# Delta levels: the upper chunk's products issued one PSUM bank behind the lower chunk's

## The reference, cut to what matters

```
a = jnp.einsum('bhnid,bhnjd->bhnij', k_beta, kc) * decay_strict
t_inv = lax.linalg.triangular_solve(eye + a, eye, left_side=True, lower=True, unit_diagonal=True)
u = t_inv @ (vc * bc[..., None])
w = t_inv @ (k_beta * jnp.exp(G)[..., None])
```

## Time and profile before

| | us |
|---|---|
| median of 3 executions | 2875.41 |
| lowest and highest | 2873.04, 2876.01 |
| the profiled execution, its own time | 2876.07 |
| its span, first to last instruction | 2874.3 |
| TensorE busy in the span | 2748.0 (96%) |
| VectorE, ScalarE, GpSimd busy | 1494.7, 967.8, 189.0 |
| mean granted TensorE clock | 0.972 |

### The profile page before, as it was taken

How to read it: one execution, slowest core, us unless ns; L and a number is a source line. 1 busy time by engine, 2 the same in 40 slices (tenths; PEclk the granted TensorE clock), 3 DMA queues, 4 the chain that set the end, 5 groups by cost and what they waited for, 6 DMA issues and landing times.

```text
span 2874.3 us, 42222 instructions
## 1 busy us (share of the span) xinstructions
PE 2748.0 (96%) x17756; PEld 2240.7 (78%) x17756; DVE 1494.7 (52%) x1845; ACT 967.8 (34%) x1471; POOL 189.0 (7%) x267
## 2 busy tenths in 40 slices
PE   6999999999999999999999899999999999968998
PEld 5888877687888878888777878888877777658787
DVE  6565565756565443333457644333365546755534
ACT  3222334523222332222345333222324444323322
POOL 3000000320000000000002300000010000013000
PEclk9999999989999999999999989999999999969999
DMA  7565542103566222232222012232232222100132
GB/s 287 200 218 203 191 167 72 52 18 112 202 207 220 88 85 102 86 112 88 95 80 71 3 59 90 88 108 93 90 103 74 66 74 69 61 1 3 56 103 73
DMA packets 46521, 299.68 MB, mean 104 GB/s; under 512 B 5664, under 2 KB 5792, under 8 KB 18080
## 3 DMA queue, kind: packets, MB, share of 16 engines
q1 hardware_dynamic: 37152, 230.35, 23.5%
q0 software_dynamic: 9216, 67.11, 6.5%
HBM read 295.35 MB, written 2.10 MB: 103 GB/s over the span
## 4 chain that ended last, share of the span: by engine, by line
PE 92%; DVE 5%; ACT 1%; DMA 1%; issue 1%; POOL 0%; SPq 0%; DVEq 0%; ACTq 0%
PE ps L921 18%; PE ps L922 18%; PE ps L923 18%; PE ps L1209 6%; PE ps L1210 6%; PE ps L1211 6%; PE ps L1516 2%; PE ps L1517 2%; PE ps L1518 2%; PE ps L2071 1%; PE ps L2055 1%; PE ps L2068 1%; DMA ada_first<-in_ada 1%; PE ps L1331 1%; PE ps L1295 1%
## 5 line engine op out<-in xcount | busy, mean ns | idle before, releaser
L921 PE MATMUL ps<-hn_hi,w_hi 128*128 128x512 f32 x1440 | 564.5, 392 | 16.9 <-DVE hn_lo L870 16.7
L922 PE MATMUL ps<-hn_lo,w_hi 128*128 128x512 f32 x1440 | 563.4, 391 | 0.0
L923 PE MATMUL ps<-hn_hi,w_lo 128*128 128x512 f32 x1440 | 562.9, 391 | 0.0
L897 DVE TENSOR_TENSOR w_lo<-w_raw,w_hi 128x2048 fp32r<-128x2048 f32 (+2 forms) x227 | 467.8, 2061 | 162.8 <-ACT w_hi L890 162.8
L890 ACT ACTIVATE w_hi<-w_raw 128x2048 fp32r<-128x2048 f32 (+2 forms) x227 | 390.6, 1721 | 100.0 <-PE ps L1211 97.3
L1209 PE MATMUL ps<-hn_hi,w_hi 128*128 128x512 f32 x776 | 323.6, 417 | 7.7 <-DVE hn_lo L870 4.9
L921 PEld LDWEIGHTS ps<-hn_hi,w_hi 128*128 128x128 f32 x1440 | 272.3, 189 | 75.3 <-issue 18.6
L923 PEld LDWEIGHTS ps<-hn_hi,w_lo 128*128 128x128 f32 x1440 | 272.3, 189 | 57.4
L922 PEld LDWEIGHTS ps<-hn_lo,w_hi 128*128 128x128 f32 x1440 | 272.4, 189 | 56.3
L1210 PE MATMUL ps<-hn_lo,w_hi 128*128 128x512 f32 x776 | 306.4, 395 | 0.0
L1211 PE MATMUL ps<-hn_hi,w_lo 128*128 128x512 f32 x776 | 305.8, 394 | 0.0
(11 more groups left out here) (470 smaller groups left out, 3630.9 us busy)
## 6 DMA issues: line engine op xcount, KB each, us to landing
w_raw<-in_up SPq DMA_DIRECT2D x88, 1024.0 KB, 4.9
ada_w<-in_ada POOLq DMA_DIRECT2D x64, 1024.0 KB, 5.2
w_raw<-in_down SPq DMA_DIRECT2D x64, 704.0 KB, 4.1
w_raw<-in_mix_in SPq DMA_DIRECT2D x20, 1024.0 KB, 4.9
w_raw<-in_dsa_in SPq DMA_DIRECT2D x18, 1024.0 KB, 4.9
w_raw<-in_merge SPq DMA_DIRECT2D x16, 768.0 KB, 4.3
ada_first<-in_ada SPq DMA_DIRECT2D x8, 1024.0 KB, 12.4
w_raw<-in_mix_out SPq DMA_DIRECT2D x8, 1024.0 KB, 4.9
```

What stands on the lines that cost most here:

```text
L897: dve.tensor_tensor(w_lo[:, slot, 0:size], w_raw[:, slot, 0:size], w_hi[:, slot, 0:size].bitcast(F32), ALU.subtract).then_inc(w_lo_ready, 1)
L921: pe.matmul(bank, wh, x_hi[:, k], start=(k == 0), stop=False)
L922: pe.matmul(bank, wh, x_lo[:, k], start=False, stop=False)
L923: return pe.matmul(bank, wl, x_hi[:, k], start=False, stop=(k == K - 1))
```

## The change

Both level functions now go over five steps instead of four. In step q the lower chunk's products of bank q and the upper chunk's products of bank q - 1 are issued in turn. The waits for bank q stand at the head of step q, so that they also stand before the upper products of bank q - 1. The increment that tells a bank is complete follows the upper chunk's last product of that bank, in step q + 1. Step 0 has lower products alone, step 4 upper products alone. Which products are made, their operands, their banks and the number of increments are the same. The other engines' programs are the same.

```
-            for q in range(4):
-                pe.wait_ge(delta_bt_ready, 2 * i + q // 2 + 1)
-                if m:
-                    pe.wait_ge(delta_xy_ready, 4 * (i - 1) + q + 1)
-                else:
-                    pe.wait_ge(delta_start, 2 * G + q // 2 + 1)
+
+            def product(q, j, c):
+                return pe.matmul(ps[half(c), level_bank(q), j * HD:(j + 1) * HD], d.bt[half(c), m % 2, q, j],
+                                 d.xy[half(c), q, j, 0], start=True, stop=True)
+            for q in range(5):
+                if q < 4:
+                    pe.wait_ge(delta_bt_ready, 2 * i + q // 2 + 1)
+                    if m:
+                        pe.wait_ge(delta_xy_ready, 4 * (i - 1) + q + 1)
+                    else:
+                        pe.wait_ge(delta_start, 2 * G + q // 2 + 1)
                 for j in range(2):
-                    for c in range(2):
-                        last = pe.matmul(ps[half(c), level_bank(q), j * HD:(j + 1) * HD], d.bt[half(c), m % 2, q, j],
-                                         d.xy[half(c), q, j, 0], start=True, stop=True)
-                last.then_inc(delta_v1_summed, 1)
+                    if q < 4:
+                        product(q, j, 0)
+                    if q:
+                        last = product(q - 1, j, 1)
+                if q:
+                    last.then_inc(delta_v1_summed, 1)
...
-            for q in range(4):
-                pe.wait_ge(delta_v1_ready, 4 * i + q + 1)
+            for q in range(5):
+                if q < 4:
+                    pe.wait_ge(delta_v1_ready, 4 * i + q + 1)
                 for j in range(2):
-                    at = P + j * P
                     if m < LEVELS - 1:
-                        for c in range(2):
-                            pe.matmul(ps[half(c), level_bank(q), at:at + HD], d.xy[half(c), q, j, 1], d.v1[half(c), q, j],
-                                      start=True, stop=True)
-                    for c in range(2):
-                        last = pe.matmul(ps[half(c), level_bank(q), at + HD:at + 2 * HD], d.v1[half(c), q, j], d.xy[half(c), q, j, 1],
-                                         start=True, stop=True)
-                last.then_inc(delta_xy_summed, 1)
+                        if q < 4:
+                            x_product(q, j, 0)
+                        if q:
+                            x_product(q - 1, j, 1)
+                    if q < 4:
+                        y_product(q, j, 0)
+                    if q:
+                        last = y_product(q - 1, j, 1)
+                if q:
+                    last.then_inc(delta_xy_summed, 1)
```

More of the change, by code:

```diff
@@ L2059, in level_x_pe, with x_product, y_product @@
         def level_x_pe(pe, d, s, m):
             i = LEVELS * (d.group + s) + m
-            for q in range(4):
-                pe.wait_ge(delta_v1_ready, 4 * i + q + 1)
+            def x_product(q, j, c):
+                at = P + j * P
+                return pe.matmul(ps[half(c), level_bank(q), at:at + HD], d.xy[half(c), q, j, 1], d.v1[half(c), q, j],
+                                 start=True, stop=True)
+            def y_product(q, j, c):
+                at = P + j * P + HD
+                return pe.matmul(ps[half(c), level_bank(q), at:at + HD], d.v1[half(c), q, j], d.xy[half(c), q, j, 1],
+                                 start=True, stop=True)
```

## The result

The changed kernel takes 2905.3 us (median of 4 executions, 2901.5 to 2910.3), the kernel before 2875.7: a ratio of 1.0092, 95% interval 1.0064 to 1.0121, so by the ratio it is slower by about 26 us (the two medians lie 29.6 us apart). A second measurement of the same program gave 2901.7 and 1.0089 (1.0074 to 1.0104). The forecast was 2889.4, range 2880 to 2903. The side was right, the size about half of what came: the first median lies 2 us above the range, the second 1 us inside it.

The account below looks back on a forecast made before the run. The prediction took TensorE's stream to bound the kernel, with the upper tile finishing last in the delta stages. Terms 3.5 + 5.8 + 3.2 + 1.0 + 0.5 summed to 14.0 us over the median of 2875.4, giving 2889.4 us, range 2880 to 2903.

Parts of the forecast that it names:

- What bounds and what the banks do: TensorE, busy 96% of the span, bounds the kernel; each tile takes a record every 58 ns, so another bank gives nothing.
- rival of strict order: In the level stages nothing passes in TensorE's program order, so steps with one tile idle cost fully: +28 us; chance 0.10.
- (a): V straight after X, 15 times: upper tile has two banks left after the last subtraction, not one; 0.23 each, 3.5 us.
- (b): Head of X, 32 phases of levels 0 to 3: upper tile idles, then restarts slower; 0.18 each, 5.8 us.
- (c): First levels: bank 1's upper products stand behind the mask wait, and the upper tile idles in three GDN groups; 3.2 us.
- (d): Last levels: final subtraction comes up to one step late, partly hidden by the read after it; 0.12 x 8, 1.0 us.
- (e): Level 0's X in the RWKV and GDN first groups runs at half clock, nearly doubling (b) three times; 0.5 us.
- the clock as a rival only: An idling tile brings one more half-clock stretch in each of eight groups, half of it lost: 13 more, 2902; chance 0.11.

Follow-up runs that it names:

- crossed kernel: Against the kernel before, banks worked in pairs, lower products of one beside upper products of the other: 2892.8 us, ratio 1.0040.
- twin: Against the kernel before, the same pairs of banks and waits, but both halves write one bank at a time: 2895.4 us, ratio 1.0043.
- V lag: Against the kernel before, only V, a level's first product, has its upper products one bank later; X as before: 2887.4 us, ratio 1.0030.
- X lag alone: Against the kernel before, only X has its upper products one bank later, V as before: 2901.3 us, ratio 1.0063.
- half X lag behind a whole V lag: Against the kernel before, upper products one bank later in V and half a bank (one j) later in X: 2892.0 us, ratio 1.0050.
- filler: The whole change plus two unread upper products in X's first step, against the kernel before: 2906.9 us, ratio 1.0100.
- GDN alone: Against the kernel before, V and X lag by a bank in the four GDN groups only: 2890.2 us, ratio 1.0049.
- two paired kernels: Against the kernel before, banks worked in pairs, halves in different banks or in the same one: 2892.8 and 2895.4 us, ratios 1.0040 and 1.0043.
- half lag: Against the kernel before, upper products of both V and X half a bank (one j) later: 2887.9 us, ratio 1.0035.
- blocks of 8 records: Against the kernel before, no lag or moved wait; in each bank all lower products are issued, then all upper ones: 2899.8 us, ratio 1.0078.

## Why the prediction was right or wrong

**What bounds and what the banks do: right.** A tile takes a record each 58 ns alone, beside a tile in the same bank, and beside one in another. The crossed kernel and its twin show it directly. The rule of the Trainium skill (TensorEngine Tiling (Array Packing), Restrictions and Gotchas, Gotcha 1) had spoken for a gain; the runs disagree with it here: in these kernels neither the time nor the pace of records of tiles on the diagonal depends on sharing the bank.

**The rival of strict order: its price came near, its mechanism did not.** 24 to 27 us stands beside its 28. But strict order asks for bare levels of 3.6, and they are 3.38; in the timeline after, the lower tile's X record at 587.56 starts before the upper tile's last V record at 587.73. A near total is no proof of a mechanism. The Trainium skill (TensorE: Matmul & The Clock Gate, Part 3, The mechanism) has starts and ends in program order; the starts here disagree.

**The terms.** (a), 0.23 for V behind the last subtraction: the V lag's bare level of 3.15 or 3.16 against 2.92 confirms it. (b), the upper tile idle at the head of X: right in kind, shown by the record at 587.97, by the X lag alone and by the half X lag behind a whole V lag, which takes it away in bare levels; too small, 0.23 (timeline, filler) for 0.17 or 0.18, since the upper tile starts 0.41 us after the lower one and not 0.35. With 0.23 it is 7.4 us instead of 5.8. (c), (d) and (e) were then too large together: 13.4 - 3.5 - 7.4 leaves 2.5 where they had 4.7. They were not measured one by one. One stage can be read without the split: in the second profile of the whole change the first RWKV stage has the clock of before,

```profile
575.10:623.00 47.90, 44.82 (x1333) 43.86 (x1335) 29.09 (x66) 13.52 (x48) 15.27 (x19) 0.96 0.02 4
```

and is 2.9 us longer; (a) and (b) at 0.23 each make 2.8 of it (4 and 8 times), and next to nothing is left for (c), (d) and (e), which had 1.0 there. This is good to some 0.3 us: the same stage, unedited, takes 44.7 in the profile of GDN alone. The sum, 14.0, met the 13.4 at an equal clock, but that close it is partly luck: (b) was short by 1.6 us and the last three terms were over by 2.2.

**The step that failed is the sentence that held the clock as a rival only.** The sum that gives 2889.4 has the lost clock at nothing beyond (e); by the table it cost 11.0 us of 24.4, on top of the forecast instead of beside it, and its chance of 0.11 was far too low. Its price there, 1.65 us for each of eight groups, 13 us, came near, but not by its mechanism of one more stretch in every group. The first groups of the two RWKV stages have none more. The second ones, which had run at full clock, fall to 0.50 in both layers of this profile and in one of the second profile; here the second group of the first layer, before, after, and the stretch itself:

```profile
597.00:620.00 23.00, 22.23 (x738) 21.96 (x730) 15.41 (x37) 7.81 (x27) 7.88 (x10) 1.00 0.02 4
```

```profile
600.00:626.00 26.00, 24.61 (x679) 24.38 (x676) 14.11 (x34) 7.26 (x26) 7.52 (x10) 0.87 0.01 3
...
602.20:608.90 6.70, 6.41 (x113) 6.41 (x114) 2.31 (x6) 0.83 (x3) 2.97 (x5) 0.50 0.01 2
```

The rows of the clock were at hand: the stages' mean was 0.89 to 0.96, and the GDN groups were already dipping. Windows over one GDN group show it, first of the kernel before, then of the changed one with the stretch at half clock inside it:

```profile
2584.30:2611.60 27.30, 23.68 (x716) 23.02 (x711) 15.97 (x35) 8.91 (x32) 10.12 (x12) 0.94 0.02 4
```

```profile
2603.90:2633.70 29.80, 26.35 (x714) 25.77 (x711) 15.81 (x35) 8.84 (x32) 10.16 (x12) 0.89 0.02 4
...
2609.40:2616.00 6.60, 5.52 (x100) 5.55 (x102) 1.79 (x4) 0.83 (x3) 2.96 (x4) 0.50 0.01 2
```

6.6 us of a group at 0.50, where the kernel before had one such stretch of 3.2:

```profile
2591.50:2594.70 3.20, 3.20 (x68) 3.20 (x65) 0.84 (x2) 0.47 (x2) 1.24 (x2) 0.50 0.02 5
```

**What stays open** is what sets the clock's share. It isn't the length added: the two paired kernels add as much at an equal clock (13.1 and 12.9) and take only 180 and 185 us of half-clock time, although the mean clock of a GDN group is as low in them as in the changed kernel (0.88 and 0.89). It is largest with the X lag (210, 207, 213, 218) and lower with a V lag or a half lag (192 to 194). It isn't cured by filling the upper tile. A part of the loss that changes from one execution to the next lies outside the stages: in the second profile of the whole change they take 47.9, 50.7 and 109.9 us, 17.6 more than before, and the rest of its span only 2.6 us more, where the rest of the first profile's took 14. Both have some 5.5 us more between the second RWKV stage and GDN's (924.7 and 924.8 for 919.2), in dense code that was not edited. No run here separates the place where a stage ends from what the engine does in it.

## What to carry to other kernels

Before putting two small-tile streams into different banks, read the pace of one tile alone from the trace; if it is the pace of the pair, the bank is not what holds them. A lag between two in-order streams costs at every joint where only one of them has work and at every wait that now stands before the other's last piece, and both can be counted from the rows. One tile's tail hides another's head only as far as the tiles can pass each other. Price the clock too: a stage that dips to half clock between waits can pay for a change nearly twice.

## What the runs showed of the hardware that was not expected

A tile with nothing queued pays about 50 ns at its first record (0.27 against 0.22), and seems to run ahead of only some 3 to 6 unstarted records of the other (three at the head of X, with a lag of one bank or of two): in blocks of 8 records a bank of X takes 0.57 us instead of 0.47. The same program's time follows its clock by 0.36 us for each us at half clock, and moves over 17 us (2872.0 to 2889.6), nine tenths of its variance with the clock; that is more than the direct cost of this change.
